# A two-layer encoder kernel on one core: attention's variance sums go to GpSimd, weight splits move among the roots, and the first scores move ahead of the last k matmuls

## The chip, the core and the metric

The kernel runs on 1 of the 8 cores of a Trainium2 chip. The metric is the device time of one execution in microseconds (us). Engines are called PE (TensorE), DVE (VectorE), ACT (ScalarE), POOL (GpSimd) and SP (SyncE, which here only issues DMAs). Each engine runs its own queue in order, and the engines meet through semaphores.

## What is computed

Two layers (the file's DEPTH is 2) work on 1024 tokens of 1024 features in float32. A layer does this:

```python
h = rms_norm(x, norm_mix_g[l])
proj = h @ w_in[l]
q, k, v, z_b, x_c = jnp.split(proj, splits, axis=-1)
mix_a = neighbourhood_attention(q, k, v, rpb[l])       # 8 heads of 64, softmax over a window of 8x16 neighbours
mix_b = spatial_gating(z_b, gmlp_ln_g[l], gmlp_ln_b[l], w_spatial[l], b_spatial[l])
mix_c = fourier_mix(x_c)
mix = head_rms_norm(jnp.concatenate([mix_a, mix_b, mix_c], axis=-1), head_norm_g[l])
x = x + mix @ w_out[l]
h = rms_norm(x, norm_ffn_g[l])
x = x + (jax.nn.silu(h @ w_gate[l]) * (h @ w_up[l])) @ w_down[l]
```

`head_rms_norm` divides each head's 64 values by the root of their mean square plus EPS (1e-6). The attention part of it is what the change touches.

## The kernel before

**Numbers as pairs.** Every large product is done three times on PE, with each operand split into a rounded part and a rest: ACT copies the raw tile to the rounded type (`..._hi`), then DVE or POOL subtracts (`..._lo`). A weight of the projections and of the output product comes in pieces of 128x1024 numbered 0 to 33. For piece p, SP loads `w_raw`, ACT makes `w_hi` (`piece_hi`), POOL makes `w_lo` (`piece_lo`, line 662), and PE waits for POOL's count `w_ready` (`wait_piece`). Pieces 18 to 33 are the output weights.

**The end of the projections.** k is projected last, into eight PSUM banks (`project(4, ...)`). For each bank b, DVE scales it (`k_raw`, line 1330), ACT rounds it (`k_hi`, line 916), DVE makes the rest (`k_lo`, `key_rest`, line 1325).

**Attention.** The 1024 queries are 8 tiles of 128, with 8 heads each, so there are 64 pairs t = 8*tile + head, handled two at a time in a loop over i = 0 to 32 on PE. An iteration of PE does: `scores(i)` (six matmuls 64x128 by 384 keys, line 1921, for pairs 2i and 2i+1), `values(i-2)` (probabilities times v, line 1954), `turn_probs` of pairs 2i-2 and 2i-1 (transposes, line 1935), and in the first eight iterations a `turn_batch` (line 1994). `scores(i)` waits until DVE has made the logits of the pairs before (`l_made`). DVE makes logits (line 1354) from the scores and a bias; ACT takes the exponential (`probs`, line 931) and writes each head's sum to `exp_sum` (SUM); DVE and ACT copy the transposed probabilities back (lines 1364 and 943).

**The heads' norm.** A tile finished by `values` goes through six steps, each in a fixed iteration of its engine's loop: DVE copies it (line 1377), PE turns it to token-major (`turn_heads`, line 1969), ACT squares it (line 955), DVE sums the squares of each head (line 1392), POOL raises to the power -0.5 (the "root", line 689), DVE multiplies (line 1401), and PE turns it back (`turn_tokens`, line 1976). The exponential is not divided by its sum; instead the variance gets EPS times the sum squared: DVE computes `exp_sum_sq` (S2, line 1387) and adds it to the summed squares (line 1396). `exp_sum` has two buffers, so ACT's first exponential of a tile t/8 >= 2 waits for the square of the sums of the tile two before (`o_eps`).

**After the loop.** `out_early(b)` starts the output product for bank b with pieces 18, 19 and 20, in the order bank 0, `values(31)`, bank 1, `turn_tokens(6)`, bank 2, `turn_heads(7)`, bank 3, and so on. The order of everything is written out by hand in the five queues; there is no scheduler.

Of the kernel before, what the change touches and what calls it, by code (L numbers as in the profile page):

```python
# [153 lines left out]
def build(nc, x, win, wout, wom, wg, wu, wd, bias, wsp, bsp, lng, lnb, gmix, ghead, gffn, gfin,  # L154
          tw, bd, ident, out):
    ctx = ExitStack()
    with ctx:
# [494 lines left out]
        def _(pool):  # L652
# [17 lines left out]
            for l in range(DEPTH):  # L670
# [41 lines left out]
        def _(act):  # L712
# [145 lines left out]
            for l in range(DEPTH):  # L858
# [68 lines left out]
                def probs(t):  # L927
                    act.wait_ge(l_made, l * 64 + t + 1)
                    if t >= 16 and t % 8 == 0:
                        act.wait_ge(o_eps, l * 8 + t // 8 - 1)  # L930
                    nc.scalar.activation(L[:, t % 4, :], L[:, t % 4, :], ACT.Exp, scale=-1.0,
                                         bias=NM[:, t % 4:t % 4 + 1],
                                         accum_out=SUM[:, (t // 8) % 2, t % 8:t % 8 + 1]).then_inc(p_made, 1)

                for i in range(41):
                    if i < 32:
                        probs(2 * i)
# [6 lines left out]
                    if i < 32:  # L944
                        probs(2 * i + 1)
# [17 lines left out]
                    if i in (14, 27, 30, 33, 34):  # L963
                        piece_hi(l, {14: 18, 27: 19, 30: 20, 33: 21, 34: 22}[i])
# [100 lines left out]
        def _(dve):  # L1065
# [146 lines left out]
            for l in range(DEPTH):  # L1212
# [129 lines left out]

                for i in range(39):
                    if i < 32:
                        for t in (2 * i, 2 * i + 1):
                            tile, h = divmod(t, 8)
                            dve.wait_ge(s_full, l * 64 + t + 1)
                            if t >= 4:
# [939 lines left out]
```

## Time and profile before

| What | Value |
|---|---|
| median of 3 runs | 2083.04 us (2082.63 to 2083.73) |
| the profiled execution: its own time | 2083.01 us |
| its span in the trace | 2081.2 us |
| PE busy | 2056.7 us (99%), 10364 matmuls |
| DVE, ACT, POOL busy | 1435.1 (69%), 827.8 (40%), 222.5 (11%) us |
| chain that ended last | PE 92%, DVE 5%, ACT 1%, DMA 1% |

The profiled execution is 0.03 us from the median, and 1.8 us of it lie around the span. A matmul's printed duration is a model and overlaps the next one, so PE's busy share hides short stalls; they are read from the distance of starts.

### The profile page before, as it was taken

The page shows a single profiled execution, that of the slowest core. Times are in us where ns is not written, and L with a number is a line of the kernel's source. Part 1 is how long each engine was busy: PE and PEld are TensorE (multiplying, and loading weights), DVE is VectorE, ACT ScalarE, POOL GpSimd, SP SyncE. Part 2 cuts the span into 40 slices and gives each one's busy share as a digit, 9 for nine tenths or more (in the row PEclk, how much of TensorE's full clock was granted, in tenths as well). Part 3 has the DMA queues.
Part 4 walks back from the last instruction along what each step waited for, and adds up shares of the span by engine and source line. Part 5 has one row for each costly group of instructions (what it writes and reads, how often), then busy time and mean ns, then how long its engine had stood idle before and what let it go on. Part 6 is the DMA issues. An engine that isn't in the chain of part 4 may idle for free.

```text
span 2081.2 us, 27873 instructions
## 1 busy us (share of the span) xinstructions
PE 2056.7 (99%) x10364; PEld 1700.6 (82%) x10364; DVE 1435.1 (69%) x2352; ACT 827.8 (40%) x1458; POOL 222.5 (11%) x103
## 2 busy tenths in 40 slices
PE   8999999999999999999999999999999999999998
PEld 7888778887888888888898887788888888888887
DVE  6313784788877778787833338747998777777877
ACT  4221583452333333444612217734433333334443
POOL 1322024300000000000023300332000000000000
PEclk9999999999999999999999999999999999999999
DMA  5222433324433236633221314441253323384333
GB/s 183 71 91 61 142 103 123 100 71 150 149 102 106 96 112 247 208 97 97 77 86 61 102 41 143 143 142 46 86 172 132 101 102 103 115 297 126 98 97 122
DMA packets 111062, 244.55 MB, mean 118 GB/s; under 512 B 13648, under 2 KB 18640, under 8 KB 110672
## 3 DMA queue, kind: packets, MB, share of 16 engines
q1 hardware_dynamic: 97056, 214.45, 31.9%
q10 hardware_dynamic: 13872, 28.31, 3.8%
q8 instruction: 84, 1.38, 0.3%
q14 instruction: 50, 0.41, 0.1%
HBM read 191.86 MB, written 50.86 MB: 117 GB/s over the span
## 4 chain that ended last, share of the span: by engine, by line
PE 92%; DVE 5%; issue 1%; ACT 1%; DMA 1%; ACTq 0%; POOL 0%; DVEq 0%
PE bank L1777 28%; PE bank L1779 27%; PE bank L1778 27%; PE bank L1954 2%; PE bank L1935 2%; PE bank L1921 2%; DVE s_lo L1174 1%; DVE t_lo L1443 0%; PE bank L1976 0%; PE bank L1869 0%; PE bank L1880 0%; PE bank L1879 0%; DMA w_g<-in_wg 0%; PE bank L1898 0%; PE bank L1969 0%
## 5 line engine op out<-in xcount | busy, mean ns | idle before, releaser
L1777 PE MATMUL bank<-t_hi,s_hi 128*128 128x512 f32 (+1 forms) x1336 | 517.2, 387 | 1.9 <-DVE hid_cu L1556 1.0
L1778 PE MATMUL bank<-t_lo,s_hi 128*128 128x512 f32 (+1 forms) x1336 | 516.4, 387 | 0.0
L1779 PE MATMUL bank<-t_hi,s_lo 128*128 128x512 f32 (+1 forms) x1336 | 516.3, 386 | 0.0
L1777 PEld LDWEIGHTS bank<-t_hi,s_hi 128*128 128x128 f32 x1336 | 250.9, 188 | 54.5 <-DVE hid_cu L1556 1.9
L1779 PEld LDWEIGHTS bank<-t_hi,s_lo 128*128 128x128 f32 x1336 | 250.9, 188 | 51.0
L1778 PEld LDWEIGHTS bank<-t_lo,s_hi 128*128 128x128 f32 x1336 | 250.9, 188 | 50.6
L662 POOL TENSOR_TENSOR w_lo<-w_raw,w_hi 128x1024 fp32r<-128x1024 f32 x65 | 161.5, 2496 | 961.9 <-ACT w_hi L743 819.7
L1777 PE MATMUL bank<-b_hi,s_hi 128*128 128x512 f32 x528 | 205.9, 390 | 0.1
L1779 PE MATMUL bank<-b_hi,s_lo 128*128 128x512 f32 x528 | 205.5, 389 | 0.0
L1778 PE MATMUL bank<-b_lo,s_hi 128*128 128x512 f32 x528 | 205.4, 389 | 0.0
L1777 PE MATMUL bank<-h_hi,w_hi 128*128 128x512 f32 x512 | 201.0, 393 | 0.0
L1779 PE MATMUL bank<-h_hi,w_lo 128*128 128x512 f32 x512 | 199.4, 389 | 0.0
L1778 PE MATMUL bank<-h_lo,w_hi 128*128 128x512 f32 x512 | 199.3, 389 | 0.0
L779 ACT ACTIVATE s_hi<-w_u 128x512 fp32r<-128x512 f32 x142 | 89.7, 631 | 232.8 <-PE bank L1779 175.3
L779 ACT ACTIVATE s_hi<-w_down 128x512 fp32r<-128x512 f32 x154 | 97.3, 632 | 199.5 <-PE bank L1779 198.8
L1174 DVE TENSOR_TENSOR s_lo<-w_down,s_hi 128x512 fp32r<-128x512 f32 x154 | 107.6, 699 | 74.6 <-ACT s_hi L779 74.6
L779 ACT ACTIVATE s_hi<-w_g 128x512 fp32r<-128x512 f32 x142 | 89.4, 630 | 160.8 <-PE bank L1779 105.6
L1777 PE MATMUL bank<-w_hi,h_hi 128*128 128x512 f32 (+1 forms) x384 | 137.3, 358 | 9.3 <-DVE h_lo L1069 9.2
L1778 PE MATMUL bank<-w_lo,h_hi 128*128 128x512 f32 (+1 forms) x384 | 136.4, 355 | 0.0
L1779 PE MATMUL bank<-w_hi,h_lo 128*128 128x512 f32 (+1 forms) x384 | 136.3, 355 | 0.0
L743 ACT ACTIVATE w_hi<-w_raw 128x1024 fp32r<-128x1024 f32 x67 | 70.3, 1058 | 128.3 <-DMA w_raw<-in_win 107.1
L1777 PEld LDWEIGHTS bank<-b_hi,s_hi 128*128 128x128 f32 x528 | 99.1, 188 | 21.4 <-issue 0.9
(217 smaller groups left out, 3217.4 us busy)
## 6 DMA issues: line engine op xcount, KB each, us to landing
w_g<-in_wg SPq DMA_DIRECT2D x44, 512.0 KB, 3.6
w_u<-in_wu SPq DMA_DIRECT2D x44, 512.0 KB, 4.4
t_raw<-hidden_t SPq DMA_DIRECT2D x88, 256.0 KB, 2.6
bias<-in_bias SPq DMA_DIRECT2D x24, 768.0 KB, 5.3
w_raw<-in_win SPq DMA_DIRECT2D x34, 512.0 KB, 4.0
t_raw<-hidden_b SPq DMA_DIRECT2D x66, 256.0 KB, 2.6
hidden_b<-hid_g SPq DMA_DIRECT2D x60, 256.0 KB, 2.0
hidden_t<-hid_x SPq DMA_DIRECT2D x44, 256.0 KB, 2.0
```

The source lines that it names most:

```text
L662: nc.gpsimd.tensor_tensor(WL[s][:, :], WR[s][:, :], WH[s][:, :], ALU.subtract).then_inc(w_ready, 1)
L743: nc.scalar.activation(WH[s][:, :], WR[s][:, :], ACT.Copy).then_inc(w_hi, 1)
L779: nc.scalar.activation(SH[q % W_RING][:, :], weight_block(q), ACT.Copy).then_inc(s_hi, 1)
L1174: nc.vector.tensor_tensor(SL[q % W_RING][:, :], weight_block(q), SH[q % W_RING][:, :], ALU.subtract)\
L1777: nc.tensor.matmul(bank, lh, rh, start=start, stop=False)
L1778: nc.tensor.matmul(bank, lh, rl, start=False, stop=False)
L1779: return nc.tensor.matmul(bank, ll, rh, start=False, stop=stop)
L1921: mm = nc.tensor.matmul(B[e][:, 0:NKEY].rearrange("p (r c) -> p r c", c=KC), qs[hp, c, q0:q0 + P], grid(ks[hp, c, :])[:, 4 * rr:4 * rr + K ...
L1935: mm = nc.tensor.transpose(B[2 + t % 2][:, n * P:(n + 1) * P], L[:, t % 4, n * P:(n + 1) * P], IDENT[:, :])
L1954: mm = nc.tensor.matmul(B[4 + tile % 2][e * DH:(e + 1) * DH, c * P:(c + 1) * P], VB[j % 2][:, rr + n, h * DH:(h + 1) * DH], PT[:, h % 4, n ...
```

## The change

It has five parts, in both layers.

1. DVE's two small operations (lines 1387 and 1396) leave DVE. POOL now squares the sums and adds them to the squares, ahead of each root. Constants are folded: ACT's square has a scale (DH*EPS)**-0.5, and DVE's last multiply a factor EPS**-0.5.
2. On POOL, the rests of the output weights stand at other roots: piece 18 behind root 1 (was root 2), 19 behind root 5 (was root 4), 20 behind root 6 (was root 5), 21 and 22 behind root 6 as before.
3. On ACT, piece 19 is rounded in two halves in iterations 29 and 30 (was whole in 27), and piece 20 in iteration 32 (was 30).
4. `scores(0)` moves in among the matmuls of k's last bank (bank 7), and with it DVE's first two logits and ACT's first two exponentials move ahead of the handling of that bank.
5. For tile 0, DVE sums the squares ahead of two copies in iteration 8. `turn_batch(i)` waits for `k_raw` of its own bank only.

```diff
@@ pool @@
                 for t in range(8):
+                    pool.wait_ge(p_made, l * 64 + 8 * t + 8)
+                    if t:
+                        pool.wait_ge(o_var, l * 8 + t)
+                    nc.gpsimd.tensor_tensor(S2[:, :], SUM[:, t % 2, :], SUM[:, t % 2, :], ALU.mult).then_inc(o_eps, 1)
+                    pool.wait_ge(o_eps, l * 8 + t + 1)
+                    pool.wait_ge(o_red, l * 8 + t + 1)
+                    nc.gpsimd.tensor_tensor(SS[:, 0:HA], SS[:, 0:HA], S2[:, :], ALU.add).then_inc(o_var, 1)
                     pool.wait_ge(o_var, l * 8 + t + 1)
                     nc.gpsimd.tensor_tensor(SR[:, 0:HA], SS[:, 0:HA], NHALF[:, 0:HA], ALU.pow).then_inc(o_rstd, 1)
-                    if t in (2, 4, 5, 6):
-                        piece_lo(l, {2: 18, 4: 19, 5: 20, 6: 21}[t])
+                    if t in (1, 5):
+                        piece_lo(l, 18 if t == 1 else 19)
                     if t == 6:
-                        piece_lo(l, 22)
+                        for p in (20, 21, 22):
+                            piece_lo(l, p)
@@ act @@
+                for b in range(8):
+                    if b == 7:
+                        probs(0)
+                        probs(1)
+                    act.wait_ge(k_raw, l * 8 + b + 1)
...
-                    if i < 32:
+                    if 0 < i < 32:
                         probs(2 * i)
...
-                        nc.scalar.activation(B[4 + tile % 2][:, :], B[6 + tile % 2][:, :],
-                                             ACT.Square).then_inc(o_sq, 1)
+                        nc.scalar.activation(B[4 + tile % 2][:, :], B[6 + tile % 2][:, :], ACT.Square,
+                                             scale=(DH * EPS) ** -0.5).then_inc(o_sq, 1)
...
-                    if i in (14, 27, 30, 33, 34):
-                        piece_hi(l, {14: 18, 27: 19, 30: 20, 33: 21, 34: 22}[i])
+                    if i in (29, 30):
+                        s, w = ALL_SLOT[19], slice((i - 29) * 512, (i - 28) * 512)
...
+                        op = nc.scalar.activation(WH[s][:, w], WR[s][:, w], ACT.Copy)
+                        if i == 30:
+                            op.then_inc(w_hi, 1)
+                    if i in (14, 32, 33, 34):
+                        piece_hi(l, {14: 18, 32: 20, 33: 21, 34: 22}[i])
@@ dve @@
+                def logits(t):
...
                 for b in range(8):
+                    if b == 7:
+                        logits(0)
+                        logits(1)
                     dve.wait_ge(acc_full, l * 40 + 32 + b + 1)
...
+                def head_sums(tile):
+
+                    dve.wait_ge(o_sq, l * 8 + tile + 1)
+                    if tile:
+                        dve.wait_ge(o_rstd, l * 8 + tile)
+                    else:
+                        dve.wait_ge(hs_norm, l * 2 + 2)
+                    nc.vector.tensor_reduce(SS[:, 0:HA], B[4 + tile % 2][:, :].rearrange("p (h d) -> p h d", d=DH),
+                                            AX_X, ALU.add).then_inc(o_red, 1)
...
                     if i == 0:
                         key_rest(7)
+                    if i == 8:
+                        head_sums(0)
...
-                        nc.vector.scalar_tensor_tensor(out=S2[:, :], in0=s, scalar=EPS, in1=s, op0=ALU.mult,
-                                                       op1=ALU.mult).then_inc(o_eps, 1)
...
-                        nc.vector.scalar_tensor_tensor(out=SS[:, 0:HA], in0=SS[:, 0:HA], scalar=1.0 / DH,
-                                                       in1=S2[:, :], op0=ALU.mult, op1=ALU.add).then_inc(o_var, 1)
+                    if i >= 12 and i % 4 == 0:
+                        head_sums((i - 8) // 4)
...
-                        nc.vector.tensor_tensor(OT[:, :, :], B[6 + tile % 2][:, :].rearrange("p (h d) -> p h d", d=DH),
-                                                SR[:, 0:HA].rearrange("p (h a) -> p h a", a=1)
-                                                .to_broadcast([P, HA, DH]), ALU.mult).then_inc(o_norm, 1)
+                        nc.vector.scalar_tensor_tensor(
+                            out=OT[:, :, :], in0=B[6 + tile % 2][:, :].rearrange("p (h d) -> p h d", d=DH),
+                            scalar=EPS ** -0.5, in1=SR[:, 0:HA].rearrange("p (h a) -> p h a", a=1)
+                            .to_broadcast([P, HA, DH]), op0=ALU.mult, op1=ALU.mult).then_inc(o_norm, 1)
@@ pe @@
                         for k in range(4, KT_D):
+                            if g == 4 and b == 7 and k == 6:
+                                scores(0)
                             mm = product(k, b)
...
-                    pe.wait_ge(k_raw, l * 8 + 8)
+                    pe.wait_ge(k_raw, l * 8 + 7 + b % 2)
...
-                    if i < 32:
+                    if 0 < i < 32:
                         scores(i)
```

**POOL, roots 4 to 6, before.** `head_rstd` rows are the roots (root 4, 5 and 6 here); `w_lo6`, `w_lo10`, `w_lo1` and `w_lo4` are the rests of pieces 19, 20, 21 and 22.

```order
L689 TENSOR_TENSOR head_rstd_219<-head_ss_218,minus_half_216 128x8 [waits o_var] x2
L662 TENSOR_TENSOR w_lo6_96<-w_raw6_108,w_hi6_84 128x1024 [waits w_hi]
L689 TENSOR_TENSOR head_rstd_219<-head_ss_218,minus_half_216 128x8 [waits o_var]
L662 TENSOR_TENSOR w_lo10_100<-w_raw10_112,w_hi10_88 128x1024 [waits w_hi]
L689 TENSOR_TENSOR head_rstd_219<-head_ss_218,minus_half_216 128x8 [waits o_var]
L662 TENSOR_TENSOR w_lo1_91<-w_raw1_103,w_hi1_79 128x1024 [waits w_hi]
L662 TENSOR_TENSOR w_lo4_94<-w_raw4_106,w_hi4_82 128x1024 [waits w_hi]
```

The same place now, from root 5 on.

```order
L696 TENSOR_TENSOR head_rstd_219<-head_ss_218,minus_half_216 128x8 [waits o_var]
L662 TENSOR_TENSOR w_lo6_96<-w_raw6_108,w_hi6_84 128x1024 [waits w_hi]
L691 TENSOR_TENSOR exp_sum_sq_223<-exp_sum_222 128x8 [waits o_var,p_made]
L694 TENSOR_TENSOR head_ss_218<-head_ss_218,exp_sum_sq_223 128x8 [waits o_red,o_eps]
L696 TENSOR_TENSOR head_rstd_219<-head_ss_218,minus_half_216 128x8 [waits o_var]
L662 TENSOR_TENSOR w_lo10_100<-w_raw10_112,w_hi10_88 128x1024 [waits w_hi]
L662 TENSOR_TENSOR w_lo1_91<-w_raw1_103,w_hi1_79 128x1024 [waits w_hi]
L662 TENSOR_TENSOR w_lo4_94<-w_raw4_106,w_hi4_82 128x1024 [waits w_hi]
```

The rest of piece 20 (`w_lo10`) stood ahead of root 6 and now stands behind it and its two new small operations.

**PE, the end of k's last bank, before.** `bank7` rows are k's last matmuls, `bank0` and `bank1` from `k_hi`/`q_hi` are `scores(0)`, `xc_tok` is `turn_batch(0)`.

```order
L1777 MATMUL bank7<-h_hi_50,w_hi10_88 128x512
L1778 MATMUL bank7<-h_lo_51,w_hi10_88 128x512
L1779 MATMUL bank7<-h_hi_50,w_lo10_100 128x512
L1921 MATMUL bank0<-k_hi_55,q_hi_52 128x384 [waits k_lo,q_lo,const_landed]
L1921 MATMUL bank1<-k_hi_55,q_hi_52 128x384
L1921 MATMUL bank0<-k_lo_56,q_hi_52 128x384
L1921 MATMUL bank1<-k_lo_56,q_hi_52 128x384
L1921 MATMUL bank0<-k_hi_55,q_lo_53 128x384
L1921 MATMUL bank1<-k_hi_55,q_lo_53 128x384
L1994 MATMUL bank6<-ident_197,xc_tok_61 128x128 [waits k_raw,hs_norm]
```

The same place now.

```order
L1944 MATMUL bank0<-k_hi_55,q_hi_52 128x384 [waits k_lo,q_lo]
L1944 MATMUL bank1<-k_hi_55,q_hi_52 128x384
L1944 MATMUL bank0<-k_lo_56,q_hi_52 128x384
L1944 MATMUL bank1<-k_lo_56,q_hi_52 128x384
L1944 MATMUL bank0<-k_hi_55,q_lo_53 128x384
L1944 MATMUL bank1<-k_hi_55,q_lo_53 128x384
L1800 MATMUL bank7<-h_hi_50,w_hi10_88 128x512
L1801 MATMUL bank7<-h_lo_51,w_hi10_88 128x512
L1802 MATMUL bank7<-h_hi_50,w_lo10_100 128x512
L1800 MATMUL bank7<-h_hi_50,w_hi10_88 128x512
L1801 MATMUL bank7<-h_lo_51,w_hi10_88 128x512
L1802 MATMUL bank7<-h_hi_50,w_lo10_100 128x512
```

The six matmuls of `scores(0)` stood behind all of bank 7 and now stand ahead of its last six; `turn_batch(0)` and `scores(1)` follow bank 7 directly.

**DVE, iteration 8, before.** `bank4` into `head_ss` is the sum of squares of tile 0, the `ISA` rows from `bank0` and `bank1` are logits.

```order
L1354 ISA logits_75,minus_max_220<-bank1,bias0_62 128x384 [waits s_full,pt_full]
L1354 ISA minus_max_220 128x1
L1364 COPY probs_t_208<-bank2 128x384 [waits pv_done,pt_full]
L1369 SCALAR_TENSOR_TENSOR h_lo_51<-bank7,g_head_213,h_hi_50 128x512 [waits bt_hi]
L1392 TENSOR_REDUCE head_ss_218<-bank4 128x8 [waits o_sq]
L1396 SCALAR_TENSOR_TENSOR head_ss_218<-head_ss_218,exp_sum_sq_223 128x8 [waits o_red,o_eps]
L1354 ISA logits_75,minus_max_220<-bank0,bias0_62 128x384 [waits s_full,pt_full]
```

The same place now.

```order
L1357 ISA logits_75,minus_max_220<-bank1,bias0_62 128x384 [waits s_full,pt_full]
L1357 ISA minus_max_220 128x1
L1386 TENSOR_REDUCE head_ss_218<-bank4 128x8 [waits hs_norm,o_sq]
L1403 COPY probs_t_208<-bank2 128x384 [waits pv_done,pt_full]
L1408 SCALAR_TENSOR_TENSOR h_lo_51<-bank7,g_head_213,h_hi_50 128x512 [waits bt_hi]
L1357 ISA logits_75,minus_max_220<-bank0,bias0_62 128x384 [waits s_full,pt_full]
```

The sum of squares moved ahead of the two copies, and the small sum (line 1396) is gone from between it and the next logits.

## Rows read from the trace of the kernel before

**Rows 1.** The page's first line.

```profile
span 2081.2 us, 27873 instructions
```

**Rows 2.** Timeline of PE, late iterations of layer 0: start, duration, engine, line, idle before.

```profile
301.40 0.44 PE L1921 MATMUL bank<-k_hi,q_hi 64*128 64x384 f32 x2
...
303.75 0.44 PE L1921 MATMUL bank<-k_hi,q_hi 64*128 64x384 f32 x2
...
307.09 0.45 PE L1921 MATMUL bank<-k_hi,q_hi 64*128 64x384 f32 x2 [0.68 <-DVE minus_max L1354]
...
313.12 0.88 PE L1954 MATMUL bank<-probs_t,v_band 128*64 128x128 f32 x12 [0.39 <-ACT probs_t L943]
...
316.03 0.40 PE L1777 MATMUL bank<-h_hi,w_hi 128*128 128x512 f32 x1
```

**Rows 3.** Timeline of PE, iteration 10 of layer 0.

```profile
254.72 0.45 PE L1921 MATMUL bank<-k_hi,q_hi 64*128 64x384 f32 x2 [0.60 <-DVE minus_max L1354]
```

**Rows 4.** Timeline of DVE, iteration 28 of layer 0.

```profile
304.79 1.29 DVE L1396 SCALAR_TENSOR_TENSOR head_ss<-head_ss,exp_sum_sq 128x8 f32<-128x8 f32 x1
```

**Rows 5.** Timeline of all engines, the first two iterations of layer 0.

```profile
227.52 0.39 PE L1779 MATMUL bank<-h_hi,w_lo 128*128 128x512 f32 x1
...
227.95 0.69 DVE L1330 SCALAR_TENSOR_TENSOR k_raw<-bank,rstd_mix 128x512 f32<-128x512 f32 x1 [0.63 <-PE bank L1779]
...
228.67 0.64 ACT L916 ACTIVATE k_hi<-k_raw 128x512 fp32r<-128x512 f32 x1 [2.09 <-DVE k_raw L1330]
...
229.82 0.69 DVE L1325 TENSOR_TENSOR k_lo<-k_raw,k_hi 128x512 fp32r<-128x512 f32 x1
...
230.95 0.56 DVE L1354 CUSTOM_DVE_ANT_0 logits<-bank,bias 128x384 f32<-128x384 f32 x1 [0.44 <-PE bank L1921]
...
231.43 0.55 DVE L1354 CUSTOM_DVE_ANT_0 logits<-bank,bias 128x384 f32<-128x384 f32 x1
...
232.05 0.45 PE L1921 MATMUL bank<-k_hi,q_hi 64*128 64x384 f32 x2
```

**Rows 6.** Timeline of all engines, iterations 14 to 17 of layer 0.

```profile
268.88 1.05 ACT L743 ACTIVATE w_hi<-w_raw 128x1024 fp32r<-128x1024 f32 x1
...
272.19 0.61 ACT L931 ACTIVATE logits<-logits,minus_max 128x384 f32<-128x384 f32 x1 [0.22 <-DVE minus_max L1354]
...
272.92 0.44 PE L1921 MATMUL bank<-k_hi,q_hi 64*128 64x384 f32 x2
273.03 0.49 ACT L943 ACTIVATE probs_t<-bank 128x384 f32<-128x384 f32 x1
...
273.66 0.88 PE L1954 MATMUL bank<-probs_t,v_band 128*64 128x128 f32 x12
```

**Rows 7.** Timeline of all engines, iterations 31 and 32 of layer 0.

```profile
312.08 2.36 POOL L662 TENSOR_TENSOR w_lo<-w_raw,w_hi 128x1024 fp32r<-128x1024 f32 x1 [4.28 <-ACT w_hi L743]
...
314.99 0.68 DVE L1392 TENSOR_REDUCE head_ss<-bank 128x8 f32<-128x512 f32 x1
...
315.78 0.17 DVE L1396 SCALAR_TENSOR_TENSOR head_ss<-head_ss,exp_sum_sq 128x8 f32<-128x8 f32 x1
316.03 1.64 POOL L689 TENSOR_TENSOR head_rstd<-head_ss,minus_half 128x8 f32<-128x8 f32 x1 [1.58 <-DVE head_ss L1396]
...
317.63 2.41 POOL L662 TENSOR_TENSOR w_lo<-w_raw,w_hi 128x1024 fp32r<-128x1024 f32 x1
```

**Rows 8.** Groups by line on POOL: count, then busy us and mean ns.

```profile
L667 POOL TENSOR_TENSOR rstd_tok_ffn<-rstd_tok_ffn,minus_half 128x4 f32<-128x4 f32 x5 | 5.0, 1007 | 649.4 <-DVE rstd_tok_ffn L1093 615.3 <-DVE rstd_tok_ffn L1430 34.1
```

**Rows 9.** Timeline of PE, the start of the kernel.

```profile
9.21 0.55 PE L1777 MATMUL bank<-w_hi,h_hi 128*128 128x256 f32 x1 [9.21 <-DVE h_lo L1069]
...
11.91 0.34 PE L1777 MATMUL bank<-w_hi,h_hi 128*128 128x256 f32 x1
...
13.40 0.28 PE L1777 MATMUL bank<-w_hi,h_hi 128*128 128x256 f32 x1
```

**Rows 10.** One window near the end: PE, PEld, DVE, ACT, POOL busy, granted clock, DMA.

```profile
2077.00:2078.00 1.00, 0.00 (x0) 0.00 (x0) 1.00 (x3) 0.00 (x0) 0.00 (x0) 0.54 1.02 335
```

More of the change, by code:

```diff
@@ L913, in _, with probs @@
                 nc.scalar.activation(JUNK[:, :], EPS_T[:, :], ACT.Exp)
+                def probs(t):
+                    act.wait_ge(l_made, l * 64 + t + 1)
+                    if t >= 16 and t % 8 == 0:
+                        act.wait_ge(o_eps, l * 8 + t // 8 - 1)
+                    nc.scalar.activation(L[:, t % 4, :], L[:, t % 4, :], ACT.Exp, scale=-1.0,
+                                         bias=NM[:, t % 4:t % 4 + 1],
+                                         accum_out=SUM[:, (t // 8) % 2, t % 8:t % 8 + 1]).then_inc(p_made, 1)
                 for b in range(8):
+                    if b == 7:
+                        probs(0)
+                        probs(1)
                     act.wait_ge(k_raw, l * 8 + b + 1)
@@ L1326, in key_rest @@
                                             KH_[:, b // 2, half(b % 2)], ALU.subtract).then_inc(k_lo, 1)
+                def logits(t):
+                    tile, h = divmod(t, 8)
+                    dve.wait_ge(s_full, l * 64 + t + 1)
+                    if t >= 4:
+                        dve.wait_ge(pt_full, l * 64 + t - 3)
+                    if h % 4 == 0:
+                        dve.wait_ge(bias_landed[BIAS_BUF[tile]][h // 4], l * 48 + 16 * BIAS_NTH[tile])
+                    dve.sem_inc(dve_passed, 1)
+                    nc.vector.tensor_tensor_reduce(
+                        L[:, t % 4, :], B[t % 2][:, 0:NKEY], BIAS[BIAS_BUF[tile]][:, h, :], -1.0, 3e38,
+                        ALU.add, ALU.min, NM[:, t % 4:t % 4 + 1]).then_inc(l_made, 1)
                 for b in range(8):
+                    if b == 7:
+                        logits(0)
+                        logits(1)
                     dve.wait_ge(acc_full, l * 40 + 32 + b + 1)
@@ L1341, in mixed_lo @@
                                                        op0=ALU.mult, op1=ALU.subtract).then_inc(mix_lo, 1)
+                def head_sums(tile):
[6 more added lines that the diff above has]
+                                            AX_X, ALU.add).then_inc(o_red, 1)
                 for i in range(39):
                     if i < 32:
[L1345 to L1348, printed above, removed]
[L1349 to L1356 removed]
+                        if i:
+                            logits(2 * i)
+                            logits(2 * i + 1)
                     if i == 0:
                         key_rest(7)
+                    if i == 8:
+                        head_sums(0)
                     if 1 <= i < 33:
@@ L1905, in _ @@
                 project(3, lambda n, b: pe.wait_ge(mb_made if n < 4 else mc_made, l * 4 + n % 4 + 1))
-                project(4, lambda n, b: pe.wait_ge(q_raw, l * 8 + BANKS.index(b) + 1), range(8))
                 def scores(i):
@@ L1926, in scores @@
                                 mm.then_inc(s_full, 1)
+                project(4, lambda n, b: pe.wait_ge(q_raw, l * 8 + BANKS.index(b) + 1), range(8))
                 def turn_probs(t):
@@ L2022, in _ @@
                 for i in range(33):
-                    if i < 32:
+                    if 0 < i < 32:
                         scores(i)
```

31 lines of the change are left out of this document (2 added, 29 removed).

## The prediction

> **What bounds the kernel now.** I read the page first. The span is 2081.2 us [rows 1] and PE is busy nearly all of it, so only PE's stalls can be won or lost. Since printed matmul durations overlap, I went on to PE's timeline in the attention stretch of layer 0 and looked at the distance between starts. Two successive `scores` rows without extras lie 303.75 - 301.40 = 2.35 us apart [rows 2], and nearly all iterations hold that distance, so the stretch is bound by PE with four small holes. The hole before `scores(30)`: 307.09 - 303.75 = 3.34 in place of 2.35, so 1.0 us. The hole before `values(30)`: PE prints 0.39 idle, released by ACT's copy of the probabilities [rows 2]. The hole before `scores(10)`: 0.60 printed idle, released by DVE's logits [rows 3]. For its causes the timeline of DVE: in iteration 28 the sum of 8 elements (line 1396) takes 1.29 us [rows 4], a multiple of what it takes elsewhere; POOL was splitting a weight meanwhile. The fourth hole is at the start, where `scores(1)` waits for DVE. Layer 1 repeats all four. By the chain of waits and the list of waits nothing else in attention holds PE for long.
>
> **The change part by part.** All sums are for one layer and doubled at the end.
>
> *The start (part 4).* `scores(0)` will run before the last six matmuls of bank 7, so `scores(1)` no longer waits. But what is late next is `scores(2)`. DVE must do `k_lo(7)` before the logits of `scores(1)`, and bank 7 now ends later. The last matmul of bank 7 starts today at 227.52 [rows 5]. A batch of scores ahead of it takes 273.66 - 272.92 = 0.74 us [rows 6], and the changes of operand about 0.1 (an estimate), so it will start at 228.36. From there by rows 5: `k_raw` 0.43 later (227.95 - 227.52), `k_hi` 0.72 later, `k_lo` 0.67 later (the 0.64 of `k_hi` and a hand-over of 0.03), logits 0.65 later (the 0.69 of `k_lo`, with the small overlap that neighbours on DVE show), the second logits 0.48 later, PE 0.62 later (232.05 - 231.43). That is 231.93 against 232.05 now. I take a gain of 0.1 us. If `k_lo` did not hold DVE, the most to be had would be the idle of the hole, 0.8.
>
> *Iteration 8 (part 5) and the small operations (part 1).* DVE reaches its logits before `scores(10)` earlier by a reduction of 0.7 us and a small sum. That hole closes: -0.6. I count 0.7, as starts show a little more than the printed idle. The hole before `scores(30)` closes too, since no operation of DVE in the loop has two inputs in SBUF any more for POOL's weight split to hold up, and ACT has lost the whole piece 19 from iteration 27: -1.0. The half pieces in iterations 29 and 30 take some 0.55 each (half of the 1.05 of a whole one, rows 6) and fit the idle that ACT has there.
>
> *The hole before `values(30)` (part 3).* ACT's work before it shrinks from a whole piece to half of one. The copy still cannot start before the transposes end, so of the 0.39 [rows 2] I take 0.2 (bounds 0 and 0.39).
>
> *The chain of the roots (part 1).* From the end of the reduction to the root lie today a hand-over inside DVE of 0.11, 0.17 of work and 0.08 to POOL [rows 7]. Now: 0.08 to POOL, an addition of 8 elements there, and a wait for it, say 0.1. No row shows such an addition. It is bounded from below by DVE's 0.17 and from above by what is fixed in a root: 8 elements take 1.64 us [rows 7] and 4 take 1.01 [rows 8], so 0.16 an element and 0.38 fixed. I take 0.2, since an addition is no power. The root comes 0.0 us later (-0.05 to +0.2), and PE reaches most `turn_tokens` without waiting today, with a little slack: 0. The upper bound could cost about 0.1 a tile.
>
> The Trainium skill speaks against this part: its GPSIMD Engine Reference, section 4.1 Engine selection, wants elementwise work on VectorE and puts GpSimd at about half its speed for two inputs. By that rule the addition would cost 0.34, and the sum would grow by nothing that PE sees; at 8 elements what is fixed decides, and no row here shows it.
>
> *The sum's square on POOL behind piece 18 (parts 1 and 2).* This is a new wait. POOL works in order, and the square for tile 2 now stands behind the rest of piece 18, which cannot start before ACT has rounded it: 268.88 + 1.05 [rows 6], + 0.08 to POOL, + 2.4 for the split [rows 7] = 272.4. With 0.1 between, 0.2 for the square and 0.05 to ACT, ACT's exponential of pair 32 starts at 272.77 in place of 272.19 [rows 6]. Behind it ACT has the copy of pair 31 (0.61 later), which PE's `values(15)` follows by 0.63 (273.66 - 273.03). That gives 274.01 for a row that now starts at 273.66: +0.3 (bounds 0.1 and 0.6).
>
> *Piece 20 (part 2).* This is the largest term. `out_early(0)` multiplies with piece 20 at 316.03 [rows 2]. Today its rest is made from 312.08 to 314.44 [rows 7], while PE is still in iteration 31. Now it stands behind root 6, and root 6 needs the reduction of tile 6, which DVE starts 314.99 - 313.12 = 1.87 us after `values(30)`, behind a copy that itself waits for PE's last transposes. So nothing won earlier moves it relative to PE. The chain is 314.99 + 0.68 (reduction) + 0.08 + 0.20 + 0.10 (addition) = 316.05 for the root, + 1.60 (317.63 - 316.03, root to next start) = 317.65, + 2.41 (split) = 320.06, + about 0.08 to PE = 320.14 [rows 7]. ACT is no limit: piece 20 takes the place that piece 21 has there today, and the split that starts directly behind the root in rows 7 is that of piece 21, so its rounding was done. PE stands still from 316.03 to 320.14: +4.1 us (3.9 with the shortest addition, 4.4 with the longest). There is no cover for it, because PE's queue has the piece's product next and everything else behind. What follows on DVE, ACT and POOL hangs on PE there and moves with it. Pieces 21 and 22 are needed only after all eight `out_early`, many matmuls later, and the square of tile 7 waits behind them on POOL but is not late, since tile 7's reduction is delayed by the same stall.
>
> *Sum.* -0.1 - 0.7 - 1.0 - 0.2 + 0.0 + 0.3 + 4.1 = +2.4 us a layer, +4.8 for both. PE is never idle long enough elsewhere to give it back. The profiled execution took 2083.01 us, 0.03 from the median, so 2087.8.
>
> **The rivals.**
>
> *The clock falls in the stall.* The two stalls of 4 us would be the longest inside the kernel. At its start PE's first twelve matmuls of 256 columns took 11.91 - 9.21 = 2.70 us, the next twelve 13.40 - 11.91 = 1.49 [rows 9], the distances of 1.2 and 2.4 GHz; that cost 1.2 us after a wait of 9.2 us. At the end the granted clock is 0.54 in the window from 2077 [rows 10], so about the lower level when PE had nothing to do. For it: those two places. Against it: both had more or longer idleness around them. If the clock fell in both stalls, +2.4 us, 2090.2; in one, 2089.0.
>
> The Trainium skill (TensorE: Matmul & The Clock Gate, section on HAM oscillation) has the rule that a long enough wait halves the clock, which full work then wins back; by it the time would be that of this rival. The trace agrees at both ends of the kernel, and no row shows the middle.
>
> *Only the holes count.* If a step of the piece 20 chain overlapped with what I put in a row, the stall could be near 3 us and the net +1 a layer: 2085, within 0.2%. For it: the four savings are read from stalls that are surely there. Against: each step of the chain waits for the one before.
>
> *Faster.* The single mechanism is that PE does not stand at piece 20. Then the net is -2.0 + 0.3 a layer, 2079.6. It decides at the time of the rest of piece 20: the change wins if PE gets it before 317.7, that is 2.4 us sooner than worked out, which needs the reduction of tile 6 ahead of the last transposes. DVE's queue has it behind them.
>
> *The start gains fully.* 0.7 more a layer, 2086.4. Against: `k_lo(7)` stands ahead of the logits on DVE.
>
> **How the numbers follow.** A measurement of this kernel tells 0.2%, 4.2 us, from no change, so slower begins at 2087.2. Chances: the forecast (stall near 4, clock as before) 0.60, the clock falls at least once 0.20, the short stall 0.10, the full start 0.06, faster 0.04. The forecast's own spread is 2086.6 to 2089.2 by the bounds of the addition, the split and the square; I put 0.8 of it above 2087.2. Slower: 0.48 + 0.20 + 0.02 = 0.70. Same: 0.12 + 0.08 + 0.05 + 0.01 = 0.26. Faster 0.04. The range leaves out the faster case, half of the short stall and the case of two falls: 2085.8 to 2090.2.
>
> **What the changed profile would show.** PE idle of 3.9 to 4.4 us once a layer at the third product of `out_early(0)`, released by POOL's `w_lo`, with that split starting 1.6 us after a root. Holes before `scores(10)` and `scores(30)` gone, `scores(1)` not waiting and `scores(2)` waiting for DVE. Pair 32's exponential released by POOL, half a microsecond late. POOL's addition between 0.1 and 0.4 us. No small operation of over 1 us on DVE. If the granted clock has a window near 0.5 after the stall, the first rival holds. I would be wrong if PE did not wait at that product, or if the small additions on POOL took over 0.6 us, which would then stall every `turn_tokens`.

## The result, and the profile after

The changed kernel takes **2092.78 us** (median of 5 runs, 2092.11 to 2093.33), the kernel before 2083.04 us in the same rounds (2082.39 to 2083.91): a ratio of **1.0045**, 95% interval 1.0034 to 1.0056. It is slower by 9.7 us, where 4.8 were forecast, and lies outside the range. The profiled execution took 2093.33 us with this span, which answers to [rows 1]:

```profile
span 2091.4 us, 27889 instructions
```

The list of PE's waits (total us, how many, the longest) has one kind of entry that the kernel before did not have:

```profile
PE bank L1800 <- POOL w_lo L662: 7.9, 2, 4.0
```

PE's timeline shows it once a layer, at the product with piece 20. This is layer 0, the place of the last row of [rows 2]:

```profile
313.52 0.47 PE L1800 MATMUL bank<-h_hi,w_hi 128*128 128x512 f32 x1
...
319.15 0.80 PE L1800 MATMUL bank<-h_hi,w_hi 128*128 128x512 f32 x1 [4.00 <-POOL w_lo L662]
319.75 0.63 PE L1801 MATMUL bank<-h_lo,w_hi 128*128 128x512 f32 x1
320.17 0.63 PE L1802 MATMUL bank<-h_hi,w_lo 128*128 128x512 f32 x1
320.73 1.55 PE L1979 MATMUL bank<-probs_t,v_band 128*64 128x128 f32 x12
...
325.37 0.45 PE L1801 MATMUL bank<-h_lo,w_hi 128*128 128x512 f32 x1
...
333.18 0.66 PE L2001 MATMUL bank<-ident,att_tok 128*128 128x128 f32 x4
```

Two things are to be seen. The wait is there, 4.00 us long. And what follows is slow: a matmul of 512 columns prints 0.63 us where it printed 0.39 before the wait, and `values(31)` 1.55 in place of 0.88. The windows of one microsecond say why (PE, PEld, DVE, ACT and POOL busy, granted clock, DMA share, GB/s):

```profile
317.00:318.00 1.00, 0.00 (x0) 0.00 (x0) 0.51 (x1) 0.61 (x1) 1.00 (x1) 1.00 0.00 0
318.00:319.00 1.00, 0.00 (x0) 0.00 (x0) 0.00 (x0) 0.00 (x0) 1.00 (x1) 0.82 0.00 0
319.00:320.00 1.00, 0.85 (x2) 0.75 (x3) 0.00 (x0) 0.00 (x0) 1.00 (x2) 0.50 0.00 0
...
324.00:325.00 1.00, 1.00 (x4) 0.72 (x3) 0.00 (x0) 0.00 (x0) 0.00 (x0) 0.50 0.85 344
325.00:326.00 1.00, 1.00 (x6) 0.76 (x5) 0.00 (x0) 0.00 (x0) 0.00 (x0) 0.77 0.14 53
```

The granted clock fell to 0.50, the 1.2 GHz level, near the end of the wait and stayed there until 325.4, though PE was busy again from 319.15. In layer 1 it did so later and for less long:

```profile
1352.00:1353.00 1.00, 0.57 (x2) 0.52 (x3) 0.00 (x0) 0.00 (x0) 1.00 (x2) 0.94 0.00 0
1353.00:1354.00 1.00, 1.00 (x6) 0.36 (x6) 0.00 (x0) 0.00 (x0) 1.00 (x1) 0.50 0.00 0
...
1356.00:1357.00 1.00, 1.00 (x5) 0.77 (x5) 0.00 (x0) 0.00 (x0) 1.00 (x2) 0.86 0.76 164
```

What sets the wait is POOL's queue, here with the rows that answer to [rows 7]:

```profile
310.77 2.36 POOL L662 TENSOR_TENSOR w_lo<-w_raw,w_hi 128x1024 fp32r<-128x1024 f32 x1 [3.92 <-ACT w_hi L979]
313.09 0.20 POOL L691 TENSOR_TENSOR exp_sum_sq<-exp_sum 128x8 f32<-128x8 f32 x1
314.77 0.20 POOL L694 TENSOR_TENSOR head_ss<-head_ss,exp_sum_sq 128x8 f32<-128x8 f32 x1 [1.49 <-DVE head_ss L1386]
315.15 1.64 POOL L696 TENSOR_TENSOR head_rstd<-head_ss,minus_half 128x8 f32<-128x8 f32 x1 [0.17 <-POOL head_ss L694]
316.75 6.98 POOL L662 TENSOR_TENSOR w_lo<-w_raw,w_hi 128x1024 fp32r<-128x1024 f32 x3
```

The addition takes 0.20 us, the root 1.64, and only then come the rests of pieces 20, 21 and 22 in one row.

The rows of the other places of [rows 2, 3, 5, 6]:

```profile
232.72 0.45 PE L1944 MATMUL bank<-k_hi,q_hi 64*128 64x384 f32 x2 [0.71 <-DVE minus_max L1357]
...
254.69 0.45 PE L1944 MATMUL bank<-k_hi,q_hi 64*128 64x384 f32 x2
...
306.21 0.45 PE L1944 MATMUL bank<-k_hi,q_hi 64*128 64x384 f32 x2
...
312.08 0.88 PE L1979 MATMUL bank<-probs_t,v_band 128*64 128x128 f32 x12 [0.23 <-ACT probs_t L955]
```

```profile
272.58 0.61 ACT L927 ACTIVATE logits<-logits,minus_max 128x384 f32<-128x384 f32 x1 [0.64 <-POOL exp_sum_sq L691]
```

The holes before `scores(10)` and `scores(30)` are gone, `scores(1)` waits for nothing, and pair 32's exponential waits for POOL, 0.4 us late. No operation of a few elements on DVE takes over 1 us any more.

A table of starts gives the terms. A shift is the start after minus the start before; a step is the shift minus that of the row above it, and for the first row minus the 0.75 of the next sentence. PE comes into this attention stretch of layer 0 already 0.75 us late (the last of the matmuls ahead of `scores(0)` starts at 226.91, the one with the same place before at 226.16).

| place, layer 0 | shift | step | forecast |
|---|---|---|---|
| `scores(2)` | 0.67 | -0.08 | -0.1 |
| `scores(10)` | -0.03 | -0.70 | -0.7 |
| `scores(18)` | 0.14 | +0.17 | +0.3 |
| `scores(30)` | -0.88 | -1.02 | -1.0 |
| `values(30)` | -1.04 | -0.16 | -0.2 |
| product with piece 20 | 3.12 | +4.16 | +4.1 |
| `turn_tokens(7)` | 6.14 | **+3.02** | 0 |

Layer 0 sums to +5.4. The start was forecast at 231.93, which is 232.68 with the 0.75, and measured 232.72. Six rows out of seven lie within 0.13 of their forecast, and the seventh was a zero that measured 3. Layer 1 adds 3.9. With the 0.75 of the start that is 10.1 of the 10.3 us between the two profiled executions.

The 0.75 has nothing to do with the change: PE's matmul number 101, far ahead of any edit, starts at 23.47 us where it started at 22.73. PE's first matmuls run at the low clock in either kernel, and in this execution 28 of them did:

```profile
8.70 0.55 PE L1800 MATMUL bank<-w_hi,h_hi 128*128 128x256 f32 x1 [8.70 <-DVE h_lo L1088]
...
14.81 0.30 PE L1801 MATMUL bank<-w_lo,h_hi 128*128 128x256 f32 x1
```

That is 6.1 us of distances of 0.21, where [rows 9] show twelve such matmuls in 2.7 us. In the 13 profiles of this study the end of that stretch lies between 11.5 and 14.8 us, with the same code there. The start itself varies too, between 8.3 and 10.0 us. By the Trainium skill (TensorE: Matmul & The Clock Gate, section What's actually happening) the number of cold matmuls at a start varies between runs of one kernel; the trace agrees, 12 and 28.

### The profile page after: what moved, and what is told of

It reads as the page before. It is cut to its first block, busy times and chain, and to the rows that moved or that the text cites. A ratio compares the mean times of both kernels' runs of the same rounds, so it can differ in the third digit from the quotient of the medians.

```text
span 2091.4 us, 27889 instructions
## 1 busy us (share of the span) xinstructions
PE 2062.4 (99%) x10364; PEld 1704.8 (82%) x10364; DVE 1424.2 (68%) x2320; ACT 829.3 (40%) x1460; POOL 228.1 (11%) x135
## 4 chain that ended last, share of the span: by engine, by line
PE 92%; DVE 5%; issue 1%; ACT 1%; POOL 1%; DMA 0%; ACTq 0%; DVEq 0%; POOLq 0%
PE bank L1800 27%; PE bank L1802 27%; PE bank L1801 27%; PE bank L1979 3%; PE bank L1960 2%; PE bank L1944 2%; DVE s_lo L1193 1%; DVE t_lo L1466 0%; PE bank L2001 0%; PE bank L1894 0%; PE bank L1905 0%; PE bank L1904 0%; DMA w_g<-in_wg 0%; PE bank L1923 0%; POOL head_rstd L696 0%
## 5 line engine op out<-in xcount | busy, mean ns | idle before, releaser
L1800 PEld LDWEIGHTS bank<-h_hi,w_hi 128*128 128x128 f32 x512 | 96.8, 189 | 30.0 <-POOL w_lo L662 8.8
```

Of the source, the lines that this page charges most:

```text
L1800: nc.tensor.matmul(bank, lh, rh, start=start, stop=False)
```

## The experiments

Each was measured beside the kernel before, whose median was 2083.1 to 2083.2 us. No run undoes part 3, 4 or 5 of the change by itself, so their terms rest on the starts above.

### Is it the clock? Work in the wait

```
                     for n in range(3):
+                        if b == 0 and n == 2:
+                            for r in range(5):
+                                out_product(OUT_P, OUT_ORDER[0], 1, 0, 1, True, True)
                         wait_piece(OUT_P + n)
```

> The changed kernel, with five more products of three matmuls ahead of the wait for piece 20, once a layer; their results are written over and enter nothing. They take 5 x 0.69 = 3.4 of the 4.0 us in which PE waits, and leave every other order as it is. Theory A, the clock: the 4.6 us above the forecast (3.0 in layer 0, 1.6 in layer 1) are matmuls at the lower clock after the wait. With PE at work in the wait the clock stays up, no window after it shows a granted clock near 0.5, the rest of the wait is 0.5 to 0.7 us, and the time is 2092.8 - 4.6 = 2088.2. Theory B, the wait itself costs more than the chain of the roots explains: the clock does not matter and the time stays at 2092.8.

Measured: **2088.43 us**, ratio 1.0026 [1.0016, 1.0035]. PE reaches the product as late as ever, but it works meanwhile. Its timeline, and the windows behind:

```profile
317.27 0.39 PE L1802 MATMUL bank<-h_hi,w_lo 128*128 128x512 f32 x1
318.32 0.50 PE L1800 MATMUL bank<-h_hi,w_hi 128*128 128x512 f32 x1 [0.66 <-POOL w_lo L662]
318.65 0.39 PE L1801 MATMUL bank<-h_lo,w_hi 128*128 128x512 f32 x1
318.88 0.40 PE L1802 MATMUL bank<-h_hi,w_lo 128*128 128x512 f32 x1
319.21 0.88 PE L1979 MATMUL bank<-probs_t,v_band 128*64 128x128 f32 x12
```

```profile
318.00:319.00 1.00, 0.68 (x3) 0.49 (x3) 0.00 (x0) 0.00 (x0) 1.00 (x2) 1.00 0.00 0
319.00:320.00 1.00, 1.00 (x14) 0.64 (x12) 0.00 (x0) 0.00 (x0) 1.00 (x1) 1.00 0.06 16
```

The clock stays at 1.00, `values(31)` takes 0.88 again, and 15 matmuls of useless work a layer make the kernel 4.35 us faster (2092.78 - 2088.43). This settles theory A: nearly half of the loss is the clock, and the order by itself costs 5.2 us, where the forecast had 4.8. The other executions say the same: the mean granted clock over the whole span is 0.998 or 0.999 in all ten of this kernel, as in those of the kernel before, and 0.996 in all five of the changed kernel.

### Is the wait at piece 20 the whole loss?

```
-                    if t in (1, 5):
-                        piece_lo(l, 18 if t == 1 else 19)
-                    if t == 6:
-                        for p in (20, 21, 22):
-                            piece_lo(l, p)
+                    for p in {1: (18,), 5: (19, 20), 6: (21, 22)}.get(t, ()):
+                        piece_lo(l, p)
```

and on ACT the half pieces for piece 19 in iterations 26 and 27 and for piece 20 in iterations 29 and 30.

> The changed kernel with piece 20 made ready earlier: ACT rounds piece 19 in halves in iterations 26 and 27 and piece 20 in halves in iterations 29 and 30, and POOL makes both rests behind root 5, so only pieces 21 and 22 stand behind root 6. Theory A, piece 20 is the whole loss: no wait of PE at the third product of out_early(0), no fall of the clock, and the five small terms stay as measured (-0.1, -0.7, +0.2, -1.0, -0.2 a layer): 2083.0 - 3.6 = 2079.4. Theory B, something else of the change costs as well and was hidden behind the stall (roots or heads late on POOL): 2081 or more, with a wait of PE for DVE or POOL between out_early(0) and turn_tokens(7).

Measured: **2079.96 us**, ratio 0.9984 [0.9976, 0.9993]. No wait for `w_lo` is left in the list, and the five other terms stand as in the table. Theory A holds. POOL in layer 0:

```profile
306.24 2.38 POOL L662 TENSOR_TENSOR w_lo<-w_raw,w_hi 128x1024 fp32r<-128x1024 f32 x1
310.20 2.36 POOL L662 TENSOR_TENSOR w_lo<-w_raw,w_hi 128x1024 fp32r<-128x1024 f32 x1 [1.58 <-ACT w_hi L977]
```

The rest of piece 20 ends at 312.6 and PE multiplies with it at 314.40.

### The move alone, on the kernel before

```
-                    if t in (2, 4, 5, 6):
-                        piece_lo(l, {2: 18, 4: 19, 5: 20, 6: 21}[t])
-                    if t == 6:
-                        piece_lo(l, 22)
+                    for p in {2: (18,), 4: (19,), 6: (20, 21, 22)}.get(t, ()):
+                        piece_lo(l, p)
```

> The kernel before with one edit: POOL makes the rest of piece 20 behind root 6 and not behind root 5. Theory A: the same stall of 4.1 us and the same fall of the clock as in the changed kernel, 1.6 to 3.0 us a layer: 2 x 4.1 + 4.6 = 12.8, so 2095.8. Theory B, the clock falls only together with other parts of the change: 2091.2. Theory C, without the savings ahead of it the stall is shorter since root 6 is not tied to PE's progress: under 2090.

Measured: **2094.56 us**, ratio 1.0057 [1.0044, 1.0069]. One piece in another place costs 11.4 us. PE waits 3.82 us at the product, which starts 4.0 us late against `scores(31)`, and the clock falls in both layers:

```profile
320.88 0.50 PE L1775 MATMUL bank<-h_hi,w_hi 128*128 128x512 f32 x1 [3.82 <-POOL w_lo L662]
```

```profile
321.00:322.00 1.00, 1.00 (x5) 0.59 (x7) 0.00 (x0) 0.00 (x0) 1.00 (x1) 0.85 0.00 0
322.00:323.00 1.00, 1.00 (x12) 0.92 (x10) 0.00 (x0) 0.00 (x0) 1.00 (x1) 0.50 0.07 16
```

This is theory A. What comes behind the product, nearly all of it the clock, is 1.6 us in either layer (`turn_tokens(7)` is 5.6 us later against `scores(31)`, the product 4.0). The theory had twice 4.1 and 4.6, so its sum was 1.2 us high. Theory C falls: where nothing is saved ahead of it, the wait is only 0.2 us shorter.

### Shorter waits

The five products of the first experiment became one in layer 0 and two in layer 1:

```
-                            for r in range(5):
+                            for r in range(1 + l):
```

> The changed kernel with one product of three matmuls ahead of the wait for piece 20 in layer 0 and two in layer 1 (five in the run before), whose results enter nothing. POOL's chain is the same, so PE still gets the piece at the same time, but waits only 4.0 - 0.7 = 3.3 us in layer 0 and 4.0 - 1.4 = 2.6 us in layer 1. Theory A, a wait under about 3.5 us does not bring the clock down: 2088.4, as with five products, and no granted clock under 1 behind the waits. Theory B, any wait of this order does: 1.5 to 3.0 us a layer more, about 2092. Between them, the clock falls in layer 0 alone: about 2090.2.

Measured: **2091.99 us**, ratio 1.004 [1.0027, 1.0054]. Theory A falls: waits of 3.31 and 2.52 us brought the clock down too. The first window is in layer 0, where PE was back at work from 317.92; the others show the shorter wait, in layer 1:

```profile
319.00:320.00 1.00, 1.00 (x13) 0.67 (x11) 0.00 (x0) 0.00 (x0) 1.00 (x1) 0.66 0.07 16
...
1349.00:1350.00 1.00, 0.10 (x1) 0.10 (x1) 0.00 (x0) 0.00 (x0) 1.00 (x2) 1.00 0.00 0
1350.00:1351.00 1.00, 1.00 (x3) 0.52 (x3) 0.00 (x0) 0.00 (x0) 1.00 (x1) 0.57 0.00 0
```

The five runs reach from 2088.25 to 2093.20, far wider than those of any other kernel here, and their mean granted clocks say why. The run of 2088.25, which is the time of the kernel with the filled wait, has 0.999, as that kernel has: the clock did not fall in it. The profiled run of 2090.50 has 0.997, and the three others, from 2091.99 up, 0.996. So waits of this length bring the clock down in most executions, not in all, and how long it stays down varies. What decides that stays open.

Then three and four products:

```
-                            for r in range(5):
+                            for r in range(3 + l):
```

> The changed kernel with three products of three matmuls ahead of the wait for piece 20 in layer 0 and four in layer 1, whose results enter nothing: waits of 1.9 and 1.3 us. Waits of 3.3 and 2.5 us brought the clock down behind them, one of 0.66 us did not. Theory A, a wait under 2 us leaves the clock up in both layers: 2088.4. Theory B, it falls in layer 0 alone: about 2089.9. Theory C, in both: about 2091.5.

Measured: **2089.07 us**, ratio 1.0028 [1.0017, 1.0039]. Theory A: after waits of 1.94 and 1.19 us no window shows less than 1.00, and the mean granted clock of all eight runs is 0.998 or 0.999. The longer wait:

```profile
319.21 0.50 PE L1800 MATMUL bank<-h_hi,w_hi 128*128 128x512 f32 x1 [1.94 <-POOL w_lo L662]
```

```profile
319.00:320.00 1.00, 0.79 (x3) 0.49 (x3) 0.00 (x0) 0.00 (x0) 1.00 (x2) 1.00 0.00 0
320.00:321.00 1.00, 1.00 (x14) 0.73 (x13) 0.00 (x0) 0.00 (x0) 1.00 (x1) 1.00 0.06 16
```

All of these in one table, the time of PE from `scores(31)` to `turn_tokens(7)`, in which every wait for piece 20 lies, in the profiled executions:

| kernel | PE idle at piece 20, layers 0 and 1 | `scores(31)` to `turn_tokens(7)` | clock fell |
|---|---|---|---|
| before | none | 17.17, 17.18 | no |
| five products | 0.66, 0.56 | 21.40, 21.31 | no |
| three and four | 1.94, 1.19 | 21.33, 21.28 | no |
| one and two | 3.31, 2.52 | 22.90, 22.75 | both |
| changed | 4.00, 3.90 | 24.20, 22.78 | both |

The four lower kernels have the same chain on POOL and differ only in what PE does meanwhile. The kernel with five products is 4.1 to 4.2 us a layer behind the kernel before, which is the order by itself. Against it the clock adds 1.4 to 1.5 us when it falls late and 2.8 us when it falls before the wait ends.

### One place earlier on POOL

```
+                    if t == 6:
+                        piece_lo(l, 20)
                     pool.wait_ge(o_var, l * 8 + t + 1)
                     nc.gpsimd.tensor_tensor(SR[:, 0:HA], SS[:, 0:HA], NHALF[:, 0:HA], ALU.pow).then_inc(o_rstd, 1)
```

> The changed kernel with POOL's rest of piece 20 one place earlier, behind the addition of tile 6 and ahead of its root. The split then waits only for ACT's rounding, which ends at 315.7 in the profile of the changed kernel: PE gets the piece at 315.7 + 0.1 + 2.36 + 0.1 = 318.3 and not at 319.15, a wait of 3.2 us. The root comes 2.9 us later, at 318.1, which turn_tokens(6), 3.8 us behind the product, still hides. Theory A, the chain of the roots is what set the stall: 0.9 us a layer less, 2091.0 with the clock falling as in the changed kernel, 2086.5 with a clock that stays up. Theory B, the late root costs as much at turn_tokens(6): 2092.8, with a wait there.

Measured: **2091.17 us**, ratio 1.0038 [1.0026, 1.0051], theory A with a falling clock. The wait is 3.06 us, and the late root holds nobody:

```profile
318.78 0.80 PE L1802 MATMUL bank<-h_hi,w_hi 128*128 128x512 f32 x1 [3.06 <-POOL w_lo L662]
```

### What the small operations on POOL are worth

On the kernel with piece 20 early, the square and the addition went back to DVE, first with piece 18's rest behind root 1. On POOL:

```
-                    nc.gpsimd.tensor_tensor(S2[:, :], SUM[:, t % 2, :], SUM[:, t % 2, :], ALU.mult).then_inc(o_eps, 1)
...
-                    nc.gpsimd.tensor_tensor(SS[:, 0:HA], SS[:, 0:HA], S2[:, :], ALU.add).then_inc(o_var, 1)
```

and on DVE the operations of the kernel before, in their places.

> The kernel of the run with piece 20 early, with the square of the sums and the addition back on DVE, as in the kernel before. Theory A, it was the place of POOL's split and not the small operations alone that made the hole before scores(30): the splits now run from 307 to 309 and from 311 to 313, where no logits stand behind a small sum of DVE, so the hole stays closed, and the +0.2 at scores(18) is gone too: 2079.0. Theory B, small sums on DVE hold PE wherever the split is: +1.0 a layer for the hole before scores(30), 2081.4.

Measured: 2080.80 us, ratio 0.9988 [0.9979, 0.9996], 0.8 above the same kernel with them on POOL. The two intervals overlap, but the starts agree: from `scores(10)` to `scores(18)` PE takes 21.13 us here and 20.73 there. The hole before `scores(30)` did stay closed, as theory A has it, but one before `scores(17)` opened, which neither theory had. The time lies nearer to theory B. POOL, DVE and PE there:

```profile
268.80 2.37 POOL L662 TENSOR_TENSOR w_lo<-w_raw,w_hi 128x1024 fp32r<-128x1024 f32 x1 [4.44 <-ACT w_hi L741]
```

```profile
269.19 2.01 DVE L1416 SCALAR_TENSOR_TENSOR exp_sum_sq<-exp_sum 128x8 f32<-128x8 f32 x1
```

```profile
272.20 0.44 PE L1943 MATMUL bank<-k_hi,q_hi 64*128 64x384 f32 x2 [0.42 <-DVE minus_max L1347]
```

POOL's split of piece 18 runs from 268.80 to 271.17, and the square of eight elements ends when it does. The Trainium skill (GPSIMD Engine Reference, section 8, Key points) says that GpSimd shares its SBUF interfaces with VectorE, so that the two get in each other's way where a VectorE instruction has two SBUF inputs. The trace agrees: 2.01 us here against 0.16 for the same square where POOL does not split.

Next, with piece 18's rest behind root 2, as before the change, the same pair of kernels. With the small operations on POOL:

```
-                    for p in {1: (18,), 5: (19, 20), 6: (21, 22)}.get(t, ()):
+                    for p in {2: (18,), 5: (19, 20), 6: (21, 22)}.get(t, ()):
```

> The kernel of the run with piece 20 early, with piece 18's rest back behind root 2. The square of tile 2's sums then stands ahead of it on POOL. Theory A, that queue is the +0.17 a layer at scores(18): it goes, 2080.0 - 0.3 = 2079.7, and ACT's exponential of pair 32 no longer waits for POOL. Theory B, the exponential is late by what ACT itself has to do there: +0.17 stays.

Measured: 2079.64 us, ratio 0.9984 [0.9975, 0.9993]. The shift at `scores(18)` is gone (theory A): from `scores(10)` to it PE takes 20.54 us, 0.19 less. In time that is 0.3 us, less than the runs scatter. And with them on DVE:

> The kernel with piece 20 early and piece 18 behind root 2, with the square of the sums and the addition on DVE, as in the kernel before. With piece 18 behind root 1 the DVE version was held for 2.0 us by POOL's split (a hole before scores(17)). Theory A, without that meeting the small operations are worth nothing on either engine: 2079.6, no hole before scores(17) or scores(30). Theory B, moving them to POOL is worth something by itself: 2080.5 or more, with a small operation over 1 us on DVE and a wait of PE for minus_max behind it.

Measured: 2079.39 us, ratio 0.9981 [0.9972, 0.999], theory A in its time and its holes. But the small operations still meet splits, twice a layer. POOL splits from 309.04 to 311.40, and DVE shows:

```profile
309.87 1.57 DVE L1416 SCALAR_TENSOR_TENSOR exp_sum_sq<-exp_sum 128x8 f32<-128x8 f32 x1
```

The other takes 1.28 us at 318.35. Neither holds PE, since no logits that PE waits for stand behind them. So the small operations are worth the same on either engine where PE does not wait behind the meeting, and part 1 of the change bought nothing that moving the splits does not buy. The runs moved ACT's rounding of piece 19 together with its split. That the hole before `scores(30)` was the split's doing is read from the row of DVE, 1.29 us in [rows 4] and at most 0.18 for every such sum here.

### The start

On the kernel with piece 20 early and piece 18 behind root 2:

```
-                    if i == 0:
+                    if i == 1:
                         key_rest(7)
```

> The kernel with piece 20 early and piece 18 behind root 2, and k_lo(7) on DVE behind the logits of scores(1) in place of ahead of them (nothing reads it before scores(3)). Theory A, k_lo(7) is what makes scores(2) wait 0.71 us in the changed kernel: 0.7 us a layer less, 2079.7 - 1.4 = 2078.3. Theory B, the logits are late because bank 7 and its k_raw end late: the wait stays at 0.3 or more, and scores(3) waits for k_lo: no gain, 2079.7.

Measured: **2078.82 us**, ratio 0.9978 [0.997, 0.9987], the fastest kernel of the study, 4.3 us under the kernel before. Half of theory A: the wait at `scores(2)` is gone, and `values(1)` has one for DVE's copy, which stands behind `k_lo(7)` now. The gain is 0.3 us a layer in the starts, not 0.7 (from `scores(0)` to `scores(10)` 27.14 us in place of 27.47):

```profile
231.86 0.44 PE L1942 MATMUL bank<-k_hi,q_hi 64*128 64x384 f32 x2
...
232.93 0.88 PE L1977 MATMUL bank<-probs_t,v_band 128*64 128x128 f32 x12 [0.27 <-DVE probs_t L1401]
```

One more place later, behind that copy:

```
                         nc.vector.tensor_copy(PT[:, t % 4, :], B[2][:, 0:NKEY]).then_inc(pt_dve, 1)
+                    if i == 1:
+                        key_rest(7)
```

> As the run with k_lo(7) behind the logits of scores(1), with k_lo(7) one place later still, behind the copy of pair 0's probabilities. There the wait of 0.71 us at scores(2) had become one of 0.27 us at values(1) for that copy. Theory A, the copy comes 0.6 us sooner and the wait is gone: 0.3 us a layer, 2078.8 - 0.6 = 2078.2. Theory B, the wait moves on to scores(3) or to the next logits: 2078.8.

Measured: 2078.92 us, ratio 0.9979 [0.9971, 0.9988], no gain: theory B in its time. The wait for DVE went, but 0.18 us of idle time stayed at `values(1)` that the profile puts down to nothing. What it is stays open.

## Why the prediction was wrong

**The chain of piece 20 was right.** Forecast: root at 316.05, split 1.60 later, PE 4.1 us late. Measured 4.16, with each link near its price (addition 0.20 of 0.20, the wait for it 0.17 of 0.10, root 1.64). The runs with the move alone, the move undone, and the move by one place (3.2 us forecast, 3.22 by the starts 315.56, where the product would have begun, and 318.78) show it from three sides.

**The small terms were right**: five of them, none off by more than 0.13 us. The largest error is the square behind piece 18, +0.17 for +0.3.

**The step that failed is the clock.** The prediction's likeliest case held that PE could stand still for 4 us in the middle of the kernel and go on at full speed, so the sum had nothing for it, and the fall got a chance of 0.20 because the two places in the trace had "more or longer idleness around them". It fell in both layers and took 2.8 and 1.5 us, 4.3 of the 4.35 us that filling the wait gave back. It also fell behind waits of 3.3 and 2.5 us.

The argument against the fall was wrong in its own trace. For the end of the kernel the prediction quotes only the window from 2077. PE's last matmuls and the window ahead of it are:

```profile
2074.60 0.68 PE L2174 MATMUL bank<-ident,rstd_tok_ffn 128*128 128x128 f32 x4 [1.56 <-DVE out_t L1126]
```

```profile
2076.00:2077.00 1.00, 0.00 (x0) 0.00 (x0) 1.00 (x4) 0.00 (x0) 0.00 (x0) 1.00 0.81 268
```

PE works until 2075.28, and a granted clock of 0.54 over the window from 2077 means that it fell within its first tenth. So the clock fell 1.8 us after PE's last work, behind a wait of 1.56 us and 0.68 us of work: about 3.4 us of idleness in all, less than the 4.1 us that the prediction worked out for the stall. The rule of the Trainium skill that the prediction cited for the rival (TensorE: Matmul & The Clock Gate, section on HAM oscillation) is the way it went: the clock halved at the long waits, and full work won it back.

**The rival's size was wrong too.** It was priced at 1.2 us a fall, from twelve slow matmuls in [rows 9], which gave 2090.2 for two falls, still 2.6 below the measured time. The falls cost 2.8 and 1.5. The stretch at the low clock is no fixed number of matmuls: 12 in one start and 28 in another, 6.2 us from 319.15 to 325.4 in layer 0 and some 3.5 us in layer 1. The price of a stretch is a little under half its length, and it was read from the start with the fewest slow matmuls of the 13 profiles. With the right price the rival would have given 2087.8 + 4.3 = 2092.1.

**A reading that did no harm.** The prediction says that no operation of DVE in the loop has two inputs in SBUF any more. The rest of k's last bank (`k_lo<-k_raw,k_hi`, at 231.02) still has two, but POOL's first split in this attention starts at 269.96.

**What remains.** The kernel with the filled wait took 2088.43 us, 0.6 above the forecast. The starts show 0.4 of it: the product is 4.2 us late against `values(30)`, for 4.1, and between it and `turn_tokens(7)` PE takes 11.19 us in place of 11.01, against 0.1 more gained in the holes, so 0.2 a layer. The rest is less than the start of the kernel varies by.

**The faster rival** named its condition rightly: piece 20 before 317.7. The run that meets it took 2079.96 us for a forecast of 2079.6, though it got there by moving the split on POOL and not the reduction on DVE.

## What to carry to other kernels

A wait of a few microseconds on a busy TensorE can have two prices, its length and a stretch at half clock behind it: here 1.4 to 2.8 us on top of 2.5 to 4.0 us, in all but one of the executions with such waits. Where the wait cannot be removed, matmuls on data that is already there, into a bank that is written over anyway, buy back the second price. And before an operation is moved to another engine because it is slow, look at what the other engine does just then: here moving the neighbour's split by one root was worth as much.

## What the runs showed of the hardware

- The granted clock may fall after the wait has ended: in the changed kernel's layer 1 PE resumed at 1352.43, and the matmul of 1352.76 is the first slow one. In the kernel with one and two products PE had been back at work for over a microsecond in layer 0 (from 317.92) when the clock fell in the window from 319. The changed kernel fell inside the wait in layer 0.
- In the profiled executions the waits for piece 20 of 2.52 to 4.00 us were all followed by the low clock (eight of eight, in four kernels), those of 0.56 to 1.94 us never (four of four). Over all executions the mean granted clock shows a fall in 19 of the 20 with the longer waits. No run has a wait between 1.94 and 2.52 us.
- This is no bound on the wait alone. Near the end of the kernel, where PE has little to do, the clock fell inside a wait of 1.56 us in two of the 13 profiles. This is the kernel with the move alone:

```profile
2087.04 1.19 PE L2172 MATMUL bank<-ident,rstd_tok_ffn 128*128 128x128 f32 x4 [1.56 <-DVE out_t L1124]
```

```profile
2086.00:2087.00 1.00, 0.00 (x0) 0.00 (x0) 1.00 (x5) 0.00 (x0) 0.69 (x1) 0.69 0.81 267
```

- A DVE operation of 128x8 with two SBUF inputs takes 0.16 us and took 1.28 to 2.01 us when it met one of POOL's splits; it ended with the split.
- The first matmul starts between 8.3 and 10.0 us and the low stretch behind it ends between 11.5 and 14.8 us, with the same code. PE's matmul number 101 starts between 21.86 and 24.03, so starts of two profiles are to be compared from a common point, not from zero.
